# First attention by pairs of heads in the two halves of TensorE's array, and a new first stage: c loaded on its own, the first affines by two engines

## The reference, cut to what matters

```python
mod = c @ w_ada[l] + b_ada[l]                      # c: 1024, w_ada: 1024 x 6144
sh1, sc1, gt1, sh2, sc2, gt2 = jnp.split(mod, N_MOD, axis=-1)
h = modulate(rms_norm(x, g_pre_mix[l]), sh1, sc1)  # h * (1 + sc1) + sh1
proj = h @ w_in[l]
bg, cg, u, q, k, v, ga, gb = jnp.split(proj, split_pts, axis=-1)
y_conv = short_conv_branch(bg, cg, u, conv_w[l]) @ w_proj_conv[l]
...
# 8 heads of 64; A[t,s] = sigmoid(z_ts) * prod_{s<j<t} (1 - sigmoid(z_tj)), s < t only
z = jnp.einsum('bhqd,bhkd->bhqk', q_blk, kh).astype(jnp.float32) * inv_sqrt
a = jnp.where(mask, jnp.exp(jax.nn.log_sigmoid(z) + suffix), 0.0)
o = jnp.einsum('bhqk,bhkd->bhqd', a, vh.astype(jnp.float32))
...
merged = jax.nn.sigmoid(ga) * y_conv + jax.nn.sigmoid(gb) * y_attn
```

## Time and profile before

| what | value |
|---|---|
| median of 3 runs | 1666.12 us |
| the three runs | 1662.19, 1666.16, 1666.12 us |
| the profiled execution, its own time | 1661.73 us |
| its span, first to last instruction | 1660.0 us |
| PE busy, share of the span | 1509.3 us, 91% |
| PE weight loads busy | 1203.1 us, 72% |
| DVE busy | 825.9 us, 50% |
| ACT busy | 415.3 us, 25% |
| POOL busy | 852.9 us, 51% |
| mean granted clock | 0.965 |
| first stage, to PE's first matmul with `w_in` | 0 to 56.0 us |
| first attention, from its first score to the product with `w_proj_attn` | 221.5 to 363.5 us |

### The profile page before, as it was taken

The page is one execution under the profiler, slowest core; times in us unless marked ns, Lnnn a source line. Parts: engine busy times, 40 slices in busy tenths (PEclk is TensorE's granted clock), DMA queues, the critical chain, the costliest instruction groups (busy, mean ns, idle before and its releaser), DMA issues.

```text
span 1660.0 us, 18799 instructions
## 1 busy us (share of the span) xinstructions
PE 1509.3 (91%) x7056; PEld 1203.1 (72%) x7056; DVE 825.9 (50%) x1109; ACT 415.3 (25%) x820; POOL 852.9 (51%) x314
## 2 busy tenths in 40 slices
PE   2799999999799999999799777798997999999995
PEld 2688776768688888888688555477777888888884
DVE  4787256632631111221618787423406665566657
ACT  3101133321520100101422366432415211111112
POOL 0556443436355655565448797153143665565561
PEclk9799999999899999999899999898998999999998
DMA  9575222112223233223233221022121223323321
GB/s 334 207 262 202 90 83 69 52 59 94 76 90 101 77 101 101 83 94 102 76 115 95 69 84 52 14 82 70 51 76 52 86 92 101 101 76 101 101 76 51
DMA packets 91555, 161.82 MB, mean 97 GB/s; under 512 B 3382, under 2 KB 44258, under 8 KB 91490
## 3 DMA queue, kind: packets, MB, share of 16 engines
q1 hardware_dynamic: 88000, 153.10, 27.4%
q10 hardware_dynamic: 3489, 7.82, 1.4%
HBM read 158.82 MB, written 2.10 MB: 97 GB/s over the span
## 4 chain that ended last, share of the span: by engine, by line
PE 82%; DVE 11%; ACT 3%; POOL 2%; issue 1%; DMA 1%; ACTq 0%; DVEq 0%; POOLq 0%
PE bank L597 25%; PE bank L598 24%; PE bank L599 24%; DVE bank L1433 3%; DVE bank L1429 1%; PE bank L809 1%; POOL w_lo L536 1%; PE bank L788 1%; PE bank L722 1%; DVE smx L1752 1%; DVE x L1429 1%; PE bank L944 1%; DMA x<-in_x 1%; PE bank L1001 1%; PE bank L982 1%
## 5 line engine op out<-in xcount | busy, mean ns | idle before, releaser
L534 POOL TENSOR_SCALAR w_hi<-w_raw 128x2048 fp32r<-128x2048 f32 x120 | 230.8, 1924 | 758.9 <-PE bank L597 696.5
L536 POOL TENSOR_TENSOR w_lo<-w_raw,w_hi 128x2048 fp32r<-128x2048 f32 x120 | 559.3, 4661 | 10.0
L597 PE MATMUL bank<-ht_hi,w_hi 128*128 128x512 f32 (+1 forms) x1200 | 451.3, 376 | 15.9 <-DVE ht_lo L1429 10.1
L598 PE MATMUL bank<-ht_hi,w_lo 128*128 128x512 f32 (+1 forms) x1200 | 448.1, 373 | 0.0
L599 PE MATMUL bank<-ht_lo,w_hi 128*128 128x512 f32 (+1 forms) x1200 | 447.9, 373 | 0.0
L597 PEld LDWEIGHTS bank<-ht_hi,w_hi 128*128 128x128 f32 x1200 | 228.9, 191 | 61.9 <-issue 14.8
L598 PEld LDWEIGHTS bank<-ht_hi,w_lo 128*128 128x128 f32 x1200 | 228.8, 191 | 42.6 <-issue 0.2
L599 PEld LDWEIGHTS bank<-ht_lo,w_hi 128*128 128x128 f32 x1200 | 228.4, 190 | 42.9
L1429 DVE TENSOR_TENSOR facc<-bank,facc 128x512 f32<-128x512 f32 x104 | 72.0, 692 | 119.4 <-PE bank L599 111.1
L1433 DVE SCALAR_TENSOR_TENSOR uc<-bank,par,uc 128x511 f32<-128x511 f32 x88 | 66.0, 750 | 120.5 <-ACT uc L1401 118.9
L598 PE MATMUL bank<-w_hi,hq_lo 128*128 128x512 f32 x256 | 101.1, 395 | 0.0
(11 more groups left out here) (231 smaller groups left out, 2112.4 us busy)
## 6 DMA issues: line engine op xcount, KB each, us to landing
w_raw<-in_w_in SPq DMA_DIRECT2D x27, 1024.0 KB, 5.2
ada_w<-in_w_ada SPq DMA_DIRECT2D x48, 512.0 KB, 6.3
w_raw<-in_w_up SPq DMA_DIRECT2D x22, 1024.0 KB, 5.0
w_raw<-in_w_mlp_in SPq DMA_DIRECT2D x16, 1024.0 KB, 5.2
w_raw<-in_w_mlp_out SPq DMA_DIRECT2D x16, 1024.0 KB, 5.0
w_raw<-in_w_down SPq DMA_DIRECT2D x11, 1024.0 KB, 4.9
w_raw<-in_w_out SPq DMA_DIRECT2D x8, 1024.0 KB, 5.0
w_raw<-in_w_mem_kv SPq DMA_DIRECT2D x8, 1024.0 KB, 5.3
```

The costliest lines, as they stand in the source:

```text
L534: g.tensor_scalar(w_hi[:, r], w_raw[:, r], 1.0, 1.0, ALU.mult, ALU.mult).then_inc(slab_hi, 1)
L536: g.tensor_tensor(w_lo[:, r], w_raw[:, r], w_hi[:, r].bitcast(F32), ALU.subtract).then_inc(slab_split, 1)
L597: inc_free(pe.matmul(o, ah, bh, start=start, stop=False))
L598: pe.matmul(o, al, bh, start=False, stop=False)
```

## The change

1. **Own transfer for c.** c comes once more, as the first DMA of ACT's queue, into `c_row` (8 x 128); PE turns it into a tile of its own (`cvec`) and DVE copies 128 x 8. The products `ada_product` read `cvec`. The turning of all `rows` stays; its copy to `vec` now stands on DVE after product 8, followed by `mod_g` = (1 + b_ada) * g, 128 x 8.
2. **x goes to SP's queue**, ahead of the blocks of `w_ada`. `FIRST_NORM` is 2 instead of 5.
3. **Shift and scale** are made from the bank by three small operations, each with an operand in PSUM.
4. **First affines in turn.** DVE does those of even tiles, ACT those of odd tiles (Identity with scale and bias); ACT copies both to `ht_hi`; DVE makes both `ht_lo`. `features` waits tile by tile (`each`) and not for four tiles.
5. **First attention by pairs.** Both heads' scores of one query tile follow each other ("zz", two banks, row halves of the array), the transposes of both heads ("tt"), and the values of both into one bank ("oo", column halves). `m1` and `at1` have two halves, one per head. The order is new: per pair 8 score tiles with one gate product after half of them and one after the rest, instead of one gate product per head. DVE waits before its first write to `b1` in a pair and not before its first mask. The count of tiles falls from 88 to 84, and with `cvec` the banks of all later tiles move on by five.

```diff
-FIRST_NORM = 5
+FIRST_NORM = 2
...
+for _p in range(-1, PAIRS):
+    ATT1_ORDER += [("tt", NT * _p + _m) for _m in range(NT) if _p >= 0]
+    for _m in range(2):
+        if _p + 1 < PAIRS:
+            ATT1_ORDER += [("zz", NT * (_p + 1) + 2 * _m), ("zz", NT * (_p + 1) + 2 * _m + 1)]
+            ATT1_ORDER += [("oo", _p)] * (_m == 1 and _p >= 0) + [("g", 2 * (_p + 1) + _m)]
+        elif _m == 1:
+            ATT1_ORDER += [("oo", _p)]
...
+            sp.dma_start(x[:], A["x"].rearrange("(m p) d -> p m d", p=P)).then_inc(x_loaded, 16)
             for i in range(2 * DC):
                 ada(i)
...
+                            if m == 0 and each is not None:
+                                each(4 * s + k)
...
+            pe.wait_ge(c_loaded, 16)
+            t = Tile(T0["cvec"])
+            pe.transpose(t.ap[:, 0:DC], c_row[:], ident[0:DC, 0:DC]).then_inc(t.full, 1)
             pe.wait_ge(rows_loaded, 16 * 16)
...
-            features(T0["w_in"], 2, ht_hi, ht_lo, ready=lambda s: all_taken(NT1_T[4 * s:4 * s + 4]))
+            features(T0["w_in"], 2, ht_hi, ht_lo, each=lambda k: Tile(NT1_T[k]).wait_taken(pe))
...
+            def scores1(n):
+
+                p, qt = n // NT, n % NT
+                for j in range(2):
+                    Tile(TT["zz", n] + j).wait_free(pe)
+                for j in range(2):
+                    t = Tile(TT["zz", n] + j)
+                    o = slice(HD * j, HD * j + HD)
+                    pe.matmul(t.ap[:, 0:W1[qt]], q1[o, p, qt * P:qt * P + P], k1[o, p, 0:W1[qt]], start=True,
+                              stop=True).then_inc(t.full, 1)
+
+            def turn1(n):
+                p, kc = n // NT, n % NT
+                for j in range(2):
+                    t = Tile(TT["tt", n] + j)
                     t.wait_free(pe)
                     if kc == 0:
-                        all_taken(range(TT["z", h], TT["z", h] + NT))
+                        all_taken(TT["zz", NT * p + qt] + j for qt in range(NT))
...
+                for kc in range(NT):
+                    for j in range(2):
+                        h = 2 * p + j
+                        ins = pe.matmul(t.ap[HD * j:HD * j + HD, kc * P:T], v1[:, kc, h * HD:h * HD + HD],
+                                        at1[:, j, A1[kc]:A1[kc + 1]], start=kc == 0, stop=kc == NT - 1)
...
+            act.dma_start(c_row[:], A["c"].rearrange("(r p) -> r p", p=P)).then_inc(c_loaded, 16)
...
-            act.dma_start(x[:], A["x"].rearrange("(m p) d -> p m d", p=P)).then_inc(x_loaded, 16)
...
+            Tile(T0["ada01"]).wait_taken(act)
+            for pair in range(DC // 2):
+                c = 2 * pair + 1
+                t = Tile(NT1_T[c])
+                t.wait_full(act)
+                st.done(act.activation(t.ap[:], t.ap[:], ACT.Identity, scale=mod[:, 1, c:c + 1], bias=mod[:, 0, c:c + 1]))
+                act.wait_ge(nt1_affine, pair + 1)
+                st.done(act.copy(ht_hi[:, c - 1], Tile(NT1_T[c - 1]).ap[:]), nt1_hi)
+                act.wait_ge(act_step, st.value(act_step))
+                st.done(act.copy(ht_hi[:, c], t.ap[:]), nt1_hi)
...
+                if i == DC:
+                    t = Tile(T0["vec"])
+                    t.wait_full(v)
+                    st.after()
+                    do(v.tensor_copy(vec[:], t.ap[:, 0:V_ALL]), tile=t)
+                    stt(mod_g[:], col(V_BADA + DC, DC), 1.0, col(V_G1, DC), ALU.add, ALU.mult)
+            t = Tile(T0["ada01"])
+            t.wait_full(v)
+            tt(mod[:, 0], t.ap[:, 0:DC], col(V_BADA, DC), ALU.add)
+            tt(t.ap[:, DC:2 * DC], t.ap[:, DC:2 * DC], col(V_G1, DC), ALU.mult)
+            tt(mod[:, 1], t.ap[:, DC:2 * DC], mod_g[:], ALU.add, tile=t)
...
+            first_affine(0)
+            for pair in range(DC // 2):
+                if pair + 1 < DC // 2:
+                    first_affine(2 * pair + 2)
+                first_low(2 * pair)
+                first_low(2 * pair + 1)
...
-                    if h >= 2:
-                        Tile(TT["t", h - 2] + NT - 1).wait_full(v)
...
+                        if p and qt == 0 and j == 0:
+                            Tile(TT["tt", NT * p - 1] + 1).wait_full(v)
                         st.after()
-                        tt(b1[:, h % 2, a:a + w], t.ap[:, 0:w], p1[:, 0:w], ALU.mult, tile=t)
+                        tt(b1[:, j, a:a + w], t.ap[:, 0:w], p1[:, 0:w], ALU.mult, tile=t)
```

More of the change, by code:

```diff
@@ L240, in build @@
         mod = sb("mod", [P, 4, DC])
+        cvec = sb("cvec", [P, DC])
+        mod_g = sb("mod_g", [P, DC])
+        c_row = sb("c_row", [DC, P])
         gpost = sb("gpost", [P, 2, D])
@@ L283, in build @@
         sgb = sb("sgb", [P, DC, T], where=ph)
-        m1 = sb("m1", [P, M1W], where=ph)
+        m1 = sb("m1", [P, 2, M1W], where=ph)
         b1 = sb("b1", [P, 2, M1W], where=ph)
-        at1 = sb("at1", [P, sum(W1)], where=ph)
+        at1 = sb("at1", [P, 2, sum(W1)], where=ph)
         ph.close()
@@ L817, in _ @@
                 else:
-                    {"z": scores1, "t": turn1, "o": values1}[what](h)
-            all_taken(TT["o", h] for h in range(H1))
+                    {"zz": scores1, "tt": turn1, "oo": values1}[what](h)
+            all_taken(TT["oo", p] for p in range(PAIRS))
             for c in range(2):
@@ L1152, in _ @@
                 act.dma_start(gpost[:, j], A[name].partition_broadcast(P)).then_inc(gp_loaded[j], 16)
-            for c in range(DC):
-                act.wait_ge(nt_tmp, 2 * NB["nt1"] + c + 1)
-                st.done(act.copy(ht_hi[:, c], Tile(NT1_T[c]).ap[:]), nt_hi)
+            Tile(T0["ada01"]).wait_taken(act)
[8 more added lines that the diff above has]
+                st.done(act.copy(ht_hi[:, c], t.ap[:]), nt1_hi)
             t0 = T0["w_in"]
@@ L1188, in _ @@
                             st.done(act.activation(sgb[:, n - DC], t.ap[:], ACT.Sigmoid), tile=t)
[L1189 to L1192 removed]
+                elif what == "zz":
+                    qt = h % NT
+                    w = W1[qt]
+                    for j in range(2):
+                        t = Tile(TT["zz", h] + j)
                         t.wait_full(act)
[L1194 to L1196 removed]
+                        if h >= NT:
+                            act.wait_ge(a1_scanned, 2 * (h - NT) + j + 1)
+                        st.done(act.activation(m1[:, j, O1[qt]:O1[qt] + w], t.ap[:, 0:w], ACT.Sigmoid, scale=-SC1))
                         st.done(act.activation(t.ap[:, 0:w], t.ap[:, 0:w], ACT.Sigmoid, scale=SC1), a1_sig)
[L1198 to L1200 removed]
+                elif what == "tt":
+                    kc = h % NT
+                    if h >= NT and kc == 0:
+                        Tile(TT["oo", h // NT - 1]).wait_full(act)
+                    for j in range(2):
+                        t = Tile(TT["tt", h] + j)
                         t.wait_full(act)
[L1202 to L1204 removed]
+                        st.done(act.copy(at1[:, j, A1[kc]:A1[kc + 1]], t.ap[:, kc * P:T]), tile=t)
                 else:
[L1206 removed]
+                    split_head(TT["oo", h], yt_hi, None, h)
             for m in range(DC):
@@ L1497, in post_and_norm @@
                         inv()
-            t = Tile(T0["vec"])
+            t = Tile(T0["cvec"])
             t.wait_full(v)
-            do(v.tensor_copy(vec[:], t.ap[:, 0:V_ALL]), tile=t)
+            do(v.tensor_copy(cvec[:], t.ap[:, 0:DC]), tile=t)
             def ada_product(i):
@@ L1779, in _ @@
                                 t if last else None)
[L1780 removed]
+                    lo_of_head(TT2["oo", n], ht_hi, ht_lo, None, CC + n, PAIRS + n + 1)
                 elif what == "l" and n == 0:
```

107 lines of the change are left out of this document (35 added, 72 removed).

## The result

The changed kernel took 1636.24 us, the median of four runs (1633.27 to 1636.55). The kernel before took 1665.57, the median of four (1662.19 to 1666.16). The ratio is 0.9824, with an interval of 0.9806 to 0.9842: faster by 1.8%. The profiled execution took 1636.55 us with a span of 1634.5; the one before took 1661.73 with 1660.0. The forecast was 1640.0 for the profiled execution and 1643 for the median.

The account below looks back on a forecast made before the run. PE, holding 82% of the chain, and its waits were taken as the bound. First stage -12.3, attention work -17.9 and new waits +8.5 gave -21.7 us: 1640.0 profiled, median 1664 - 21.7, about 1643, range 1633 to 1653.

Parts of the forecast that it names:

- rival A: First attention: no port stalls that matter, DVE's 1.2 us of slack holds in all pairs; -30.2, 1634 us; chance 0.15.
- (a), the slab: First stage: slab 0 of `w_in` lands at 37 us instead of 41.00, behind 13.3 MB; POOL's split ends at 43.5.
- (b), DVE: First stage: last w_ada product until 35.7, the 2.82 us stall goes, first tile at 42.2; PE starts at 43.75, after POOL's split.
- (c): First stage, later tiles: DVE needs 2.45 us per pair of tiles, PE 2.85 at the low clock, so no further wait.
- PE's work in the attention: First attention: scores 2.0 us less per pair, values 2.2 less; gross gain about 17.9 us, bounds 1 and 19.
- New waits: First attention: PE waits for DVE's masks, held by POOL; 3.9 + 2.0 + 1.6 + 1.0 = 8.5 us, bounds 0 and 24.
- the allowance on the schedule by hand: First attention, pairs 1 to 3: 1.6 us of PE wait in the first of them, 0.5 each as a mean for the others.
- The base: Whole kernel: sum made against the profiled 1661.73 us, median forecast started from 1664, between the two levels of the runs.
- B: First stage: x ahead of w_ada gives nothing, slab 0 lands at 41 as before; gain 8.3 us, 1647 us; chance 0.12.
- D: First attention: the array halves run in turn; 16.9 us of gross lost, 6 of waits covered, about 1654 us; chance 0.07.
- C: First attention: DVE is the bound in every pair, PE waits 4 us four times; 24 instead of 8.5, 1658.5 us; chance 0.10.
- E: First attention: slower, PE waits for both heads at each pair's first transpose until the clock falls; 1674 us at 10 per pair; chance 0.02.

Follow-up runs that it names:

- the first part alone: The kernel before with only points 1 to 4 of the change, the attention head by head as before: median 1652.81 us, ratio 0.9936.
- the two runs on the overlap: The changed kernel with head 0's scores and values before head 1's, 1642.37 us; with only scores so ordered and a PE wait between heads, 1640.45 us.

## Why the prediction held, and where its steps were off

The time lay in the range, 6.8 us below the forecast of the median, and the likeliest case, PE's start by POOL and one long wait at pair 0, is what happened. By the time alone rival A (1634) lay nearer than the forecast; it is the traces, and not the time, that speak for the forecast's mechanism.

- **(a), the slab.** The mechanism held: w_ada, x, the small rows and the broadcasts came first, at a near gapless rate. It landed at 38.09, not 37. The rate was even above the 390 taken (398), but 35 us at that rate are 13.9 MB, 0.9 more than my sum had from 3 us on: most of slab 1 moved before slab 0 was whole (from 38 to 44 us only 0.3 MB more came), which I had not counted. The 39.3 by the 358 GB/s of the Trainium skill, SBUF — State Buffer, section "A bandwidth-pool intuition that's wrong", was further off; 404 over 22 us show that this figure isn't a ceiling for this core.
- **(b), DVE.** Last product until 36.56 instead of 35.7, three small operations in 0.58. That PE would wait for POOL by a little over 1 us held: the first tile's `ht_lo` was done at 43.5, the split at 44.60. So the term was -11.4 instead of -12.3. The sum took this term whole; what each of the four points gives of it is shown only in part.
- **(c)** held: with all affines on DVE, PE waited 0.26 us.
- **PE's work in the attention.** Predicted 17.9. Measured 14.2, and 5.0 lost at pair 0 by the run with the mask in the bank: 19.2, just above my bound of 19. Scores were predicted in pieces of 0.95 and 1.75 and came as 1.04 and 1.70 (0.85 and 1.70 in pair 1), so 2.7 a pair as said. That the streaming of the two heads overlaps wholly, 1.71 for one or for both, I had not assumed. Values 2.31 as said. Not foreseen: 20 transposes in a row take 2.18 instead of 2 x 1.24, 0.3 us per pair; and the kernel before waited 0.48 for DVE right behind its first transposes, so that it did have a little to lose in the stage's middle.
- **New waits**, predicted 8.5. Pair 0: 3.9 + 2.0 predicted, 3.1 + 2.0 measured. DVE ended 16.8 us after the pair's first wide score (17.05 predicted), and PE used 0.6 of the wait for the first four transposes, which I had not seen. Pairs 1 to 3: 2.6 predicted, nothing measured. The step that failed is the allowance on the schedule by hand. That schedule was right (third mask free, fourth held, DVE done 1.2 before PE; measured 1.5), but I added 1.6 for the `mg` products in pair 1 and 0.5 each as a mean. The `mg` products ran at 254.72 and 255.71, and the first mask could not start before 256.84, when ACT's sigmoids were done: they filled a wait and moved nothing.
- **The base.** The sum runs against one execution. Measured profile to profile it is -25.2 (-25.4 by the spans) against -21.7; between the medians it is -29.3, since three of the four runs before lie at 1665 or above and the profiled one at 1661.73. What makes the two levels stays open. The mean clock of an execution doesn't order them: of the later runs of the kernel before, one took 1666.40 at 0.969, one 1659.32 at 0.970 and one 1664.53 at 0.963.

Of the rivals, B fell with the first part alone, in which slab 0 landed at 38.12 and PE started at 44.66 (its own terms add up to 1646, not 1647); D with the two runs on the overlap, in which halves kept apart cost 1.6 for the values and 2.6 to 2.8 for the scores per pair; C and E since PE waits in one pair of four. A was wrong in its mechanism (the stalls matter, by 5 us) and right in three pairs.

## What to carry to other kernels

A small transfer that starts a chain of buffers can be worth more than its own latency: an engine that waits holds the buffers, and everything behind them in the queue. Look for every in-order wait on the engine that frees buffers, and for bulk transfers that nobody needs yet standing ahead of the one that ends last. Where an operation with all operands in SBUF meets a GpSimd split, lay out by hand the few instructions against the splits (here that came out within 0.8 us, and the allowance added on top was what failed), and try an operand in a bank or an earlier tile where it doesn't fit.

## What the hardware showed that I had not expected

Products on the two halves of rows overlapped wholly (1.71 for one head or for both), even where two of one half stood ahead of two of the other. Products on halves of columns with common rows overlapped wholly by turns (2.31 where apart they would take 4.60). With all of one half first they overlapped by 0.7 us (3.86), since the second half's first product started ahead of the first half's last. In both cases the product that went ahead passed three waiting records and not more; how far PE can look ahead in general was not tried. Of 32 masks with all operands in SBUF, the 13 long ones all ended just behind a GpSimd split. Twenty transposes in one run took 2.18 us, two runs of ten 2 x 1.24: single transposes start 0.109 us apart in either, and each shorter run costs 0.15 more than ten of these.
